# A mixture-of-experts stage: the norm's shift added after the gather, the token lists made in two parts, the first block begun before the second block's rows are turned

## What is computed

```python
h2 = rmsnorm(x_mid, norm_ffn) * (1 + sc2) + sh2        # sh2: the shift, one number per feature
g_logits = h2 @ w_rg + b_rg                            # 4 groups; the best one is taken
e_sel = (h2 @ w_re + b_re)[chosen group]               # 8 experts; the best two are taken
# assignments sorted by expert, each expert's rows padded to blocks of 128
for each block of 128 rows (tok, e, wt):
    xb = h2[tok]
    y = (silu(xb @ w_g[e]) * (xb @ w_u[e])) @ w_d[e]   # 1024 -> 512 -> 1024
    out[tok] += y * wt
```

## Time and profile before

| | |
|---|---|
| median of three runs | 1728.6 us |
| the profiled execution: its own time | 1726.99 us |
| its span, first to last instruction | 1724.9 us |
| mean granted clock of TensorE | 0.955 of 2.4 GHz |
| busy: PE, DVE, ACT, POOL | 92%, 68%, 48%, 11% |

### The profile page before, as it was taken

The page is one execution under the profiler, slowest core; times in us unless marked ns, Lnnn a source line. Parts: engine busy times, 40 slices in busy tenths (PEclk is TensorE's granted clock), DMA queues, the critical chain, the costliest instruction groups (busy, mean ns, idle before and its releaser), DMA issues. The chain is left out here.

```text
span 1724.9 us, 21049 instructions
## 1 busy us (share of the span) xinstructions
PE 1585.3 (92%) x7666; PEld 1303.0 (76%) x7666; DVE 1181.1 (68%) x1406; ACT 835.0 (48%) x912; POOL 185.5 (11%) x173
## 2 busy tenths in 40 slices
PE   7999899979939999999999999397999799999995
PEld 5789677767838888888888888276866588888883
DVE  7787866636368989898888988276666833434346
ACT  2412243362237788888888787242333523222222
POOL 0000000000021232323323231000000000000000
PEclk8999999989969999999999999698999899999998
DMA  8242344423178999999999997533102132323201
GB/s 320 89 155 87 103 147 156 166 74 101 46 285 284 367 369 366 372 378 371 378 367 368 366 369 281 198 110 120 50 27 71 52 100 93 99 96 97 98 25 49
DMA packets 121576, 329.88 MB, mean 191 GB/s; under 512 B 12601, under 2 KB 80313, under 8 KB 96817
## 3 DMA queue, kind: packets, MB, share of 16 engines
q1 hardware_dynamic: 110450, 312.11, 50.0%
q0 software_dynamic: 11072, 17.03, 2.9%
HBM read 333.00 MB, written 20.99 MB: 205 GB/s over the span
## 5 line engine op out<-in xcount | busy, mean ns | idle before, releaser
L1453 DVE TENSOR_TENSOR moe_expert_lo<-moe_expert_raw,moe_expert_hi 128x2048 fp32r<-128x2048 f32 x124 | 281.2, 2289 | 57.5 <-ACT moe_expert_hi L1275 57.5
L1275 ACT ACTIVATE moe_expert_hi<-moe_expert_raw 128x2048 fp32r<-128x2048 f32 x124 | 234.8, 1920 | 25.4 <-PE moe_bank L1548 24.0
L1535 PE MATMUL moe_bank<-moe_expert_lo,moe_x_hi 128*128 128x512 f32 x512 | 202.6, 396 | 0.0
L1536 PE MATMUL moe_bank<-moe_expert_hi,moe_x_lo 128*128 128x512 f32 x512 | 199.7, 390 | 0.0
L1537 PE MATMUL moe_bank<-moe_expert_hi,moe_x_hi 128*128 128x512 f32 x512 | 199.7, 390 | 0.0
L1865 ACT ACTIVATE second_c_hi<-second_c_raw 128x2048 fp32r<-128x2048 f32 x44 | 84.0, 1909 | 162.5 <-PE second_bank L2320 161.2
L2318 PE MATMUL second_bank<-second_cx_lo,second_c_hi 128*128 128x512 f32 x352 | 141.0, 400 | 15.4 <-DVE second_cx_lo L2015 10.2
L827 PE MATMUL mixer_bank<-mixer_h_lo,mixer_w_hi 128*128 128x512 f32 x320 | 132.2, 413 | 10.7 <-DVE mixer_h_lo L577 10.7
L2319 PE MATMUL second_bank<-second_cx_hi,second_c_lo 128*128 128x512 f32 x352 | 138.5, 393 | 0.0
L2320 PE MATMUL second_bank<-second_cx_hi,second_c_hi 128*128 128x512 f32 x352 | 138.3, 393 | 0.0
L2318 PE MATMUL second_bank<-g_lo,second_c_hi 128*128 128x512 f32 x320 | 127.4, 398 | 1.2 <-DVE g_lo L2153 1.2
(11 more groups left out here) (405 smaller groups left out, 3186.2 us busy)
## 6 DMA issues: line engine op xcount, KB each, us to landing
moe_expert_raw<-in_w_exp_up_dram SPq DMA_DIRECT2D x64, 1024.0 KB, 7.6
moe_expert_raw<-in_w_exp_down_dram SPq DMA_DIRECT2D x62, 1024.0 KB, 7.3
second_c_raw<-in_w_mlp_dram SPq DMA_DIRECT2D x32, 1024.0 KB, 5.3
moe_shared<-in_w_exp_gate_dram SPq DMA_DIRECT2D x31, 1024.0 KB, 7.1
work<-in_w_exp_gate_dram SPq DMA_DIRECT2D x31, 1024.0 KB, 7.1
mixer_raw<-in_w_in_dram SPq DMA_DIRECT2D x18, 1024.0 KB, 5.1
mixer_raw<-in_w_mod_t_dram SPq DMA_DIRECT2D x16, 1024.0 KB, 4.9
second_c_raw<-in_w_in_dram SPq DMA_DIRECT2D x8, 1024.0 KB, 8.7
```

The costliest lines, as they stand in the source:

```text
L1275: act_e.activation(w_hi[q][:], raw[r], ACT.Copy).then_inc(hi_done, 1)
L1453: dve.tensor_tensor(w_lo[q][:], raw[r], w_hi[q][:].bitcast(F32), ALU.subtract)\
L1535: pe.matmul(out, x_hi[s][:, c, :], lo[:, k, :], start=(h == 0 and k == 0), stop=False)
L1536: pe.matmul(out, x_lo[s][:, c, :], hi[:, k, :], start=False, stop=False)
```

## The change

Five things. (1) In the mixer's tail the router's products are done inside the next tile, after its chunk 5, one tile late rather than two or three, and `sq_sum` is summed inside the last tile after chunk 6; ACT makes the first `xs` of a unit before the `hi` of the unit two ahead. (2) The shift is no longer added to `h2_rows`: ACT writes them scaled by `r_std`, in 8 pieces by token, SP stores each quarter at once and only then fetches weight unit 4, and the shift is added in `x_high` and `x_low`, which become 8 instructions of 128 columns each, since it differs by chunk. (3) The lists are made first for each expert's first 128 rows (32 blocks); blocks, lists and experts past these are worked out inside the first two blocks of turn 0 of the loop, which is written out once (`late_blocks`, `late_ones`, `late_lists`, `late_experts`), and PE makes that list in bank 6, so it waits there for `rows_ready` before down of block 1. SP fetches with constant indices for 14 turns. (4) PE does the gate of block 0 before it turns the rows of block 1; ACT and DVE are ordered to suit. (5) POOL clears old semaphores after the first gathers, and gathers straight from the list's column.

```diff
+                if s >= 22:
+                    residual(2 * (s - 22))
                 if s + 2 < NS:
                     high(s + 2)
                 if s == 20:
                     for c in range(4):
                         merged_high(c)
                 if s >= 22:
-                    residual(2 * (s - 22))
...
                             ins = feature_chunk(dst[:], s, k, h_hi, h_lo, c)
+                            if s >= 22 and c == 5 and 2 * (s - 22) + k >= 1:
+                                router(2 * (s - 22) + k - 1)
+                            if s == NS - 1 and k == 1 and c == 6:
+                                pe.wait_ge(rsum_done, KC - 2)
+                                squares(sq_sum, True, False)
                     ins.then_inc(acc_ready, 1)
                     if s == 22 and k == 0:
                         pe.wait_ge(shift_ready, 1)
                         pe.wait_ge(read_act, reads_upto("act", LAST0 - 1))
                         pe.matmul(bank[6][:, 0:36], ones[:], shift_sum, start=True, stop=True).then_inc(offset_ready, 1)
-                    if s > 22:
-                        router(2 * (s - 22) + k - 2)
...
-            router(KC - 2)
-            for part, (sem_of, count, src) in enumerate(((rsum_done, KC - 2, sq_sum), (rsq_done, KC, sq_new[1]))):
-                pe.wait_ge(sem_of, count)
-                for t in range(TC):
-                    ins = pe.matmul(bank[5][:, t:t + 1], src[:, 128 * t:128 * t + 128], ones[:, 0:1],
-                                    start=(part == 0 and t == 0), stop=(part == 1 and t == TC - 1))
-            ins.then_inc(rssq_ready, 1)
+            pe.wait_ge(rsq_done, KC)
+            squares(sq_new[1], False, True).then_inc(rssq_ready, 1)
             router(KC - 1).then_inc(rlogits_ready, 1)
...
-        shift = sb("shift", [P, D])
+        shift = sb("shift", [P, KC])
...
+            for t in range(TC):
+                sp.wait_ge(xst_evac, 2 * t + 2)
+                sp.dma_start(dram["h2"][t * 128:(t + 1) * 128, :], h2_rows[:, t, :]).then_inc(h2_stored, 16)
             expert_unit(None, 4, wg, 1, 0)
-            for t in range(TC):
-                sp.wait_ge(h2_ready, t + 1)
-                sp.dma_start(dram["h2"][t * 128:(t + 1) * 128, :], h2_rows[:, t, :]).then_inc(h2_stored, 16)
             for n in range(2, 4):
                 expert_unit(4 + n, (4 + n) % RAW, wu, 1, n % 2)
...
+            with sp.Fori(0, 14) as i:
+                for s in range(2):
+                    block_units(i, s, 2 * i + s, 2 * i + s + 2)
             sp.wait_ge(experts_done, 1)
-            last = sp.value_load(last_i[0:1, 0:1], min_val=1, max_val=NB_MAX // 2 - 1)
-            with sp.Fori(0, last) as i:
+            last = sp.value_load(last_i[0:1, 0:1], min_val=15, max_val=NB_MAX // 2 - 1)
+            with sp.Fori(14, last) as i:
...
+            pool.wait_ge(h2_stored, 16 * TC)
+            pool.wait_ge(first_rows_ready, 1)
+            for b in range(2):
+                gather_rows(b, tok_i[:, b:b + 1])
+            pool.wait_ge(xt_ready, 1)
+            gather_rows(0, tok_i[:, 2:3])
             for s in past_sems:
...
-            for c in range(KC):
-                act_e.wait_ge(xst_ready, c + 1)
-                act_e.activation(h2_rows[:, :, 128 * c:128 * c + 128],
-                                 bank[4 + c % 4][:].rearrange("p (t d) -> p t d", t=TC), ACT.Copy)\
-                     .then_inc(xst_evac, 1)
-            act_e.wait_ge(tables_ready, 1)
             act_e.activation(ones_r[:], ones[:], ACT.Copy)
-            act_e.activation(below_r[:], below[:], ACT.Copy).then_inc(tables_ready, 1)
+            act_e.wait_ge(below_ready, 1)
+            act_e.activation(below_r[:], below[:], ACT.Copy).then_inc(copies_ready, 1)
+            for n in range(2 * TC):
+                act_e.wait_ge(xst_ready, n + 1)
+                act_e.activation(h2_rows[:, n // 2, 512 * (n % 2):512 * (n % 2) + 512], bank[4 + n % 4][:], ACT.Identity,
+                                 scale=r_std[:, n // 2:n // 2 + 1]).then_inc(xst_evac, 1)
             act_e.sem_inc(y_s, 1)
...
-                act_e.activation(x_hi[s][:, 0:4, :], bank[0][:], ACT.Copy)
-                act_e.activation(x_hi[s][:, 4:8, :], bank[1][:], ACT.Copy).then_inc(xhi_done, 1)
+                for c in range(KC):
+                    act_e.activation(x_hi[s][:, c, :], bank[c // 4][:, 128 * (c % 4):128 * (c % 4) + 128], ACT.Identity,
+                                     bias=shift[:, c:c + 1]).then_inc(xhi_done, 1)
...
-            first_hi(2)
-            first_hi(3)
             act_e.wait_ge(gd_ready, 1)
             act_e.activation(gexp[:], gexp[:], ACT.Exp)
             act_e.activation(e2[:], e2[:], ACT.Exp).then_inc(gexp_ready, 1)
+            first_hi(2)
+            act_e.wait_ge(shift_landed, 16)
             x_high(0, 0)
+            first_hi(3)
+            split_hi(0, 0, 0)
             x_high(1, 1)
-            split_hi(0, 0, 0)
-            act_e.wait_ge(experts_done, 1)
-            last = act_e.value_load(last_i[0:1, 0:1], min_val=1, max_val=NB_MAX // 2 - 1)
+            split_hi(0, 0, 1)
             act_e.wait_ge(unit_used, SPLIT + 2)
             silu(0, 0)
-            split_hi(0, 0, 1)
             split_hi(0, 0, 2)
...
-            def token_rows(t):
-                dve.scalar_tensor_tensor(out=h2_rows[:, t, :], in0=h2_rows[:, t, :], scalar=r_std[:, t:t + 1],
-                                         in1=shift[:], op0=ALU.mult, op1=ALU.add).then_inc(h2_ready, 1)
-
-            dve.wait_ge(xst_evac, KC)
-            dve.wait_ge(shift_landed, 16)
-            token_rows(0)
...
+            slots(slot_one[:, 0:4, :], rank[:, 0:4]).then_inc(ones_ready, 1)
+            slots(slot_one[:, 4:8, :], rank[:, 4:8]).then_inc(ones_ready, 1)
...
+            def late_blocks():
+                counts = upto[:, :, 7:8].rearrange("p e o -> p (e o)")
+                step(dve.tensor_scalar(more[:], counts, 128.0, None, ALU.is_gt))
+                for j in range(2, TC):
...
+                step(dve.tensor_tensor(late_one[:], iota_row[:, 1:17].unsqueeze(1).to_broadcast([P, 8, 16]),
+                                       blk[:].unsqueeze(2).to_broadcast([P, 8, 16]), ALU.is_equal))
+
+            def late_ones():
+                for j, code in enumerate((tok_code, row_code)):
+                    dve.tensor_tensor(late_val[:, :, j, :], late_one[:], code[:].unsqueeze(2).to_broadcast([P, 8, 16]),
+                                      ALU.mult)
+                slots(slot_late[:], slot[:]).then_inc(late_ready, 1)
+
+            def late_lists():
+                dve.wait_ge(late_listed, 1)
+                dve.tensor_scalar(tok_i[:, 32:48], bank[6][:, 0:16], 1024.0, None, ALU.add)
+                dve.tensor_scalar(row_i[:, 32:48], bank[6][:, 16:32], 2048.0, None, ALU.add).then_inc(rows_ready, 1)
+
+            def late_experts():
+                step(dve.tensor_tensor(le[:], more_end[0:1, :].unsqueeze(1).to_broadcast([1, 16, 32]),
...
-                dve.wait_ge(xhi_done, b + 1)
-                dve.tensor_tensor(x_lo[s][:, 0:4, :], bank[0][:].rearrange("p (c t) -> p c t", c=4),
-                                  x_hi[s][:, 0:4, :].bitcast(F32), ALU.subtract)
-                dve.tensor_tensor(x_lo[s][:, 4:8, :], bank[1][:].rearrange("p (c t) -> p c t", c=4),
-                                  x_hi[s][:, 4:8, :].bitcast(F32), ALU.subtract).then_inc(xlo_done, 1)
+                for c in range(KC):
+                    dve.wait_ge(xhi_done, KC * b + 4 * (c // 4) + 4)
+                    ins = dve.scalar_tensor_tensor(out=x_lo[s][:, c, :],
+                                                   in0=bank[c // 4][:, 128 * (c % 4):128 * (c % 4) + 128],
+                                                   scalar=shift[:, c:c + 1], in1=x_hi[s][:, c, :].bitcast(F32),
+                                                   op0=ALU.add, op1=ALU.subtract)
+                ins.then_inc(xlo_done, 1)
...
+            dve.wait_ge(shift_landed, 16)
+            x_low(0, 0)
             first_lo(2)
-            token_gates()
-            x_low(0, 0)
-            x_low(1, 1)
             first_lo(3)
             split_lo(0, 0, 0)
+            x_low(1, 1)
             split_lo(0, 0, 1)
...
+                    for part in once[2 * s:2 * s + 1]:
+                        part()
                     gated(1 - s, b + 1, SPLIT + unit(i, s, 3) + 1)
...
+            turns(0, (late_blocks, late_ones, late_lists_and_experts, token_gates))
+            dve.wait_ge(experts_done, 1)
+            last = dve.value_load(last_i[0:1, 0:1], min_val=15, max_val=NB_MAX // 2 - 1)
+            with dve.Fori(1, last) as i:
+                turns(i)
...
-            transpose_x(1, 0)
             for h in range(2):
                 pe.wait_ge(lo_done, RAW + h + 1)
                 gate_like(bank[2][:], 0, h, h).then_inc(unit_used, 1)
+            transpose_x(1, 0)
...
+            def late_list():
+                pe.wait_ge(late_ready, 1)
```

(68 more changed lines are left out.)

146 lines of the change are left out of this document (67 added, 79 removed).

## The result

The changed kernel takes 1746.1 us (median of 4 runs, 1744.5 to 1746.3) against 1728.7 beside it (4 runs, 1727.9 to 1731.0): ratio 1.0095, 95% interval 1.0079 to 1.0111. It is 17.5 us slower where 11.4 were forecast (1740.0), and lies 0.1 above the range. The profiled execution took 1746.18, its span 1744.4, at a mean granted clock of 0.951.

What follows compares the result with a forecast made beforehand. PE was taken to bound the experts' loop without a gap, so time could come only from its ends. Mixer +3.8, down of block 1 +6.6 and clock +1.7 made +12.1 on 1726.99: forecast 1740, range 1732 to 1746, reaching down to 1730.

Steps and rivals of the forecast that it cites:

- PE's wait for `xs` 0: Mixer, unit 22's second tile: the first router waits for `x_mid` 0 and ACT's scaling until 436.9, +2.1 us.
- the one at the bank: Before down of block 1: PE waits 5 to 5.5 us at bank 6 until DVE's `late_lists` are done.
- The first gate: Start of the experts: stores and gather come earlier, so the first gate matmul comes at 515.5, 3.6 us earlier.
- my 9: First gather, ahead of block 0: competing with weights, it takes 9 us, where it took 6.4 before.
- Down of block 1: Experts' first blocks: DVE's late work delays its start from 561.07 to 567.7, +6.6; low clock behind, +1.7.
- my 2.3: Block 1 in the experts: PE's lead from the earlier first gate is 2.3 us.
- DVE's late work finds room: Rival, first blocks: the bank's wait and its clock go, so 1730 to 1731, same or a little slower; chance 0.12.
- The mixer: Mixer's end, new order of routers and sum of squares: +3.8 us in sum, bounds +0 to +5.5.
- I take half, +0.9: Mixer, behind the first router's wait: a low clock cost 1.7 after one gap, none after another; half taken.
- one sum and router 7, 0.95 each: Mixer, behind the last tile: these remain after 475.04, so 3.6 us to the logits for 5.5 before, -1.9.
- the three groups: Mixer, before the last tile's end: three more groups of eight records on PE at 0.9 each, +2.7 us.
- The bounds that I gave: Whole kernel: range from 1732 to 1746, reaching down to 1730 to hold 8 in 10.

Runs made afterwards that it cites:

- the list in bank 3: Changed kernel with PE's late list made in bank 3, the wait for `rows_ready` moved ahead of block 3's gate: 1740.1 us, ratio 1.0076.
- the late work's move: Changed kernel with all late work done before `x_low` of block 0, where DVE waits for the gathered rows: 1733.5 us, ratio 1.0042.
- the stores': Changed kernel with the four row stores issued behind two weight units (2 MB) and not five (5 MB): 1738.6 us, ratio 1.0061.

## Why the prediction was right or wrong

**Direction and mechanisms: right in the main.** PE's wait for `xs` 0, the shorter way to the first gate, the wait at the second gate unit of block 2 (2.4 forecast, 2.24), the one at the bank (5 to 5.5, 4.61), DVE without idle ahead of it, and the loop at 17.70 all stand in the profile.

**The first gate: right.** 35.6 after the start forecast, 35.1 measured. The stores land 15.0 us after issue behind 5 MB; a MB takes 2.4 us, as in the sum. The gather took 7.6 from issue to the turn, between my 9 and the 6.4 of the kernel before, so the loop's median of 9.3 was the wrong row to lean on wholly. The Trainium skill (DMA: Bandwidth & Descriptors, Queues, rings and completion order) has an engine take turns between its queues by packet, and the trace agrees with that only in part: the gather took 1.2 longer than before. Eight narrow `x_high` take 2.17, `x_low` 2.16, forecast 2.2 each. The estimate from the Trainium skill (ScalarE: Activation LUTs, What ACT_TABLE_LOAD costs) was 2.4 for the eight of ACT, and the measured 2.17 decides.

**Down of block 1: right.** +6.6 forecast, +6.9 measured; the clock behind it +1.7 against +2.1 (13.01 from down to the next turn, 10.89 before). Sum 8.3 against 9.0. The lead ahead of it was smaller than my 2.3: block 0's activations are turned 55.3 after the start (540.88), before 56.6, so 1.3, but the sum doesn't hang on it, as DVE sets the time of down. My reason against the rival "DVE's late work finds room" was only half right: that DVE ends the next gate's `lo` 2 us too late is so, but this binds PE only through the bank, as the list in bank 3 showed. I had priced the wait well and not asked whether its place in DVE's order was needed.

**The mixer: the mis-sized term.** +3.8 forecast; 6.4 in the first profile, 3.9 between two profiles with the same clock, 6.6 between the means of all M with the new order in place (six profiles, 56.8) and the old (five, 50.2). Two parts of it failed. "I take half, +0.9", for the clock: a fall behind router 0 costs up to 2.6, and I took the low stretch of the kernel before as fixed, though without it the old order is 2.5 faster and the new one is not. And "one sum and router 7, 0.95 each": behind the last tile I had -1.9, and the profile gives -0.8. PE waits 1.50 us there for ACT's square and then works at the low clock, so that the sum's row is 1.21 long and the logits (484.63) come 4.7 behind the last tile (479.9), not 3.6. The wait stood in my count (DVE and ACT till 475.04, PE with nothing to do); the clock behind it I put at nothing, and from the sum to the logits it is 3.1, not 2.0. In the first profile the terms come to the wait 3.3 (forecast 2.1), the fall behind it 2.6 (0.9), the three groups 2.7 (2.7), behind the last tile -0.8 (-1.9), and -1.6 for the fall at the first gap that stays away (none): 6.2 of the 6.4.

**Behind the experts: no term, which was nearly right, and yet part of the miss.** The first profile of before has an R that no other reached. Its own time, 1726.99, looks like an ordinary one all the same: its mixer and its E were on the slower side (M 51.26, where 48.75 occurs; E the longest of the three without the change). The bounds that I gave reach 1746.0; the measured medians are 1746.1 and 1745.2. By the parts of the profiles the change costs 6.6 in M and 9.1 in E (E without the late work's move or the stores': 100.1 to 101.2 with the change, 91.1 to 92.0 without), 15.7 of the 16.7 to 17.5 between the medians. Of the last 1 to 2 us some 0.5 may be the longer wait at the start of the second block; the rest I can't place.

## What to carry to other kernels

Before work is moved beside a full engine's loop, look for an idle stretch of that engine that is already being waited through: here DVE's late work, 8 us of its time, cost 11 in the loop and nothing 50 us earlier, ahead of the gathered rows. A wait for a shared bank makes one engine wait for all that stands before the release in the other's order, needed or not; price it, then move it or take another bank. And when a reordering adds even a short wait of TensorE's, price the clock behind it in full, and ask what the kernel before gains where its own fall stays away.

## What the runs showed of the hardware

The granted clock behind the same short gap of PE differs between executions of the same program: behind 2.08 us at the end of the experts it fell to 0.5 in ten profiles and stayed at 1.00 in three; behind 1.9 us at the end of unit 21 it fell in five and not in eight. A fall costs 1.6 us at either of these two places, and 1.1 to 2.6 behind router 0. Where one comes early another may stay away (changed kernel, first and second profile). What decides it these runs don't show. Two single profiles of one kernel differ by 4.3 us in a stretch that no edit touched, of which this fall is 1.6, and the kernel before spreads over 9 us (1722.4 to 1731.4 in 23 runs side by side).
